# Column tiles of 320, 384 and 352 in place of three times 352, in a four-layer streaming encoder step

## The reference

```
layer 0 mixer: z = h @ w_in (1024 -> 2048); half of it a gated spatial mix,
               half a causal convolution of width 4 and a gated recurrence; @ w_out
layer 0 MLP:   square(relu(h @ up)) @ down        (1024 -> 4096 -> 1024)
layer 1 mixer: bg, cg, xv = split(h @ w_in, 3);   (bg * conv3(cg * xv)) @ w_out
layer 1 MLP:   as in layer 0
```

## Time and profile before

| | |
|---|---|
| median of 3 executions | 2187.01 us (2185.21 to 2187.84) |
| the profiled execution, its own time | 2186.56 us |
| its span | 2184.6 us |
| TensorE (PE) busy | 2168.7 us, 99% |
| VectorE (DVE) busy | 907.4 us, 42% |
| ScalarE (ACT) busy | 666.8 us, 31% |
| GpSimd (POOL) busy | 96.3 us, 4% |
| DMA | 142.99 MB, mean 65 GB/s |
| granted TensorE clock, mean | 0.998 of 2.4 GHz |

### The profile page before, as it was taken

One profiled execution on the slowest core, in us unless ns is written; L12 is line 12 of the kernel. 1 busy time (PEld: TensorE's weight loads), 2 busy tenths in 40 slices (PEclk: granted clock), 3 DMA queues, 4 the chain that ended last, 5 costly groups with the idle time before them and its releaser, 6 DMA issues.

```text
span 2184.6 us, 31823 instructions
## 1 busy us (share of the span) xinstructions
PE 2168.7 (99%) x13629; PEld 2154.2 (99%) x13629; DVE 907.4 (42%) x1431; ACT 666.8 (31%) x1137; POOL 96.3 (4%) x115
## 2 busy tenths in 40 slices
PE   9999999999999999999999999999999999999998
PEld 8999999999999999999999999999999999999997
DVE  5766358323322322334953333493223223322336
ACT  6664345202311320333511112453013103202333
POOL 1000000000000000000033231000000000000000
PEclk9999999999999999999999999999999999999999
DMA  6111422111111111132311114221111111111132
GB/s 218 49 41 39 138 75 83 49 47 41 49 49 49 41 48 49 49 110 67 119 49 41 47 49 138 69 81 56 49 42 47 49 49 47 41 49 49 55 122 80
DMA packets 228891, 142.99 MB, mean 65 GB/s; under 512 B 5248, under 2 KB 227408, under 8 KB 228752
## 3 DMA queue, kind: packets, MB, share of 16 engines
q1 hardware_dynamic: 228304, 140.89, 21.3%
q0 software_dynamic: 416, 0.07, 0.0%
q10 hardware_dynamic: 32, 0.01, 0.0%
HBM read 119.22 MB, written 21.73 MB: 65 GB/s over the span
## 4 chain that ended last, share of the span: by engine, by line
PE 88%; DVE 2%; issue 0%; ACT 0%; DVEq 0%; ACTq 0%
PE ps L679 29%; PE ps L680 29%; PE ps L682 29%; DVE x_lo L1383 1%; DVE x_old L1372 0%; DVE f L1355 0%; PE ps L781 0%; DVE f L1339 0%; DVE f L1347 0%; DVE f L1365 0%; DVE w_all L1306 0%; PE ps L719 0%; DVE f L1434 0%; ACT tmp L945 0%; PE ps L804 0%
## 5 line engine op out<-in xcount | busy, mean ns | idle before, releaser
L679 PE MATMUL ps<-x_hi,w_all 128*128 128x352 f32 x2328 | 757.6, 325 | 1.5 <-DVE x_lo L1383 1.5
L680 PE MATMUL ps<-x_lo,w_all 128*128 128x352 f32 x2328 | 748.5, 322 | 0.0
L682 PE MATMUL ps<-x_hi,w_all 128*128 128x352 f32 x2304 | 740.3, 321 | 0.0
L679 PE MATMUL ps<-h_hi,w_all 128*128 128x352 f32 x1728 | 556.5, 322 | 0.0
L682 PE MATMUL ps<-h_hi,w_all 128*128 128x352 f32 x1728 | 555.2, 321 | 0.0
L680 PE MATMUL ps<-h_lo,w_all 128*128 128x352 f32 x1728 | 555.2, 321 | 0.0
L679 PEld LDWEIGHTS ps<-x_hi,w_all 128*128 128x128 f32 x2328 | 437.5, 188 | 5.4 <-issue 2.0
L680 PEld LDWEIGHTS ps<-x_lo,w_all 128*128 128x128 f32 x2328 | 437.6, 188 | 2.2
L682 PEld LDWEIGHTS ps<-x_hi,w_all 128*128 128x128 f32 x2304 | 432.6, 188 | 0.0
L909 ACT CAST w_all<-w_all_raw 128x1024 fp32r<-128x1024 f32 x168 | 175.5, 1045 | 522.1 <-DMA w_all_raw<-in_mlp_down_dram 317.8
L679 PEld LDWEIGHTS ps<-h_hi,w_all 128*128 128x128 f32 x1728 | 324.4, 188 | 0.4 <-DVE h_lo L1595 0.3
(11 more groups left out here) (218 smaller groups left out, 1458.0 us busy)
## 6 DMA issues: line engine op xcount, KB each, us to landing
w_all_raw<-in_mlp_up_dram SPq DMA_DIRECT2D x60, 512.0 KB, 3.9
w_all_raw<-in_mlp_down_dram SPq DMA_DIRECT2D x60, 512.0 KB, 3.9
x_save<-f SPq DMA_DIRECT2D x12, 1408.0 KB, 6.4
x_old<-x_save SPq DMA_DIRECT2D x12, 1408.0 KB, 11.5
w_all_raw<-in_c_w_in_dram SPq DMA_DIRECT2D x22, 512.0 KB, 3.8
w_all_raw<-in_w_in_even_dram SPq DMA_DIRECT2D x15, 512.0 KB, 3.8
x_rows<-in_x_prompt_dram SPq DMA_DIRECT2D x8, 512.0 KB, 7.5
w_all_raw<-in_w_out_even_dram SPq DMA_DIRECT2D x6, 512.0 KB, 3.9
```

Of the source, the lines that this page charges most:

```text
L679: nc.tensor.matmul(dst, wh, hi, start=(i == 0), stop=False)
L680: nc.tensor.matmul(dst, wh, lo, start=False, stop=False)
L682: last = nc.tensor.matmul(dst, wl, hi, start=False, stop=(i == KC - 1))
```

## The change

The three tiles become 320, 384 and 352 columns wide and begin at 0, 320 and 704. All column ranges are taken from two tables. The tiles `tmp` grow to 384 columns; `caches` and the three `row_` buffers move to the spare columns of `x_old` (which lies where `x_lo` does), and the 32 bytes of padding behind `tmp` go. The views of the spare columns of `x_hi` become 32 wide. The weights of slot "hb" lie at the same columns as before (320 + 32 = 352 + 0). The core of the diff:

```diff
+TILE0, WIDTH = (0, 320, 704), (320, 384, 352)
+COLS = [slice(c, c + w) for c, w in zip(TILE0, WIDTH)]
...
-        tmp = [place(f"tmp{t}", [P, TT], F32) for t in range(3)]
-        at_byte[0] += 32
+        tmp = [place(f"tmp{t}", [P, max(WIDTH)], F32) for t in range(3)]
...
-        caches = place("caches", [P, CACHE_ROWS], F32)
...
-        row_sq = place("row_sq", [P, 9], F32)
-        row_root = place("row_root", [P, 9], F32)
-        row_rstd = place("row_rstd", [P, 9], F32)
...
-        spare = [x_hi_raw[:, k * TS + TOK:k * TS + TOK + NJ] for k in range(KC)]
+        spare = [x_hi_raw[:, k * TS + TOK:k * TS + TS] for k in range(KC)]
...
+        spare = [x_old[:, k * TS + TOK:k * TS + TS] for k in range(4)]
+        caches = spare[0][:, 0:CACHE_ROWS]
...
+        row_sq, row_root, row_rstd = [b[:, 0:9] for b in spare[1:4]]
...
         def pt(buf, c, t):
-            c0 = c * (buf.shape[1] // KC) + t * TT
-            return buf[:, c0:c0 + TT]
+            c0 = c * (buf.shape[1] // KC) + TILE0[t]
+            return buf[:, c0:c0 + WIDTH[t]]
...
-                c = (32, 0)[t]
+                c = 32
...
         def bank(n):
-            return ps[:, n % NB, 0:TT]
+            return ps[:, n % NB, 0:WIDTH[UNITS[n].t]]
...
-            n = P if s < 2 else TT - 2 * P
+            n = P if s < 2 else WIDTH[t] - 2 * P
```

More of the change, by code:

```diff
@@ L154, in tile_pieces @@
 def tile_pieces(t):
-    lo, hi = t * TT, (t + 1) * TT
+    lo, hi = COLS[t].start, COLS[t].stop
     if hi <= SEQ:
-        return [(0, TT, lo, False)]
+        return [(0, WIDTH[t], lo, False)]
     return [(0, SEQ - lo, lo, False), (SEQ - lo, hi - SEQ, SEQ, True)]
@@ L293, in pt, with part, rstd_wide @@
         def pt(buf, c, t):
-            c0 = c * (buf.shape[1] // KC) + t * TT
-            return buf[:, c0:c0 + TT]
[L297 to L301, removed]
+            c0 = c * (buf.shape[1] // KC) + TILE0[t]
+            return buf[:, c0:c0 + WIDTH[t]]
+        def part(buf, k0, k1, t, c0=0, c1=None):
+            return tiles3(buf)[:, k0:k1, TILE0[t] + c0:TILE0[t] + (c1 or WIDTH[t])]
+        def rstd_wide(t, n, c0=0, c1=None):
+            c1 = c1 or WIDTH[t]
+            return rstd[:, TILE0[t] + c0:TILE0[t] + c1].unsqueeze(1).to_broadcast([P, n, c1 - c0])
         def vec(i, rows=P):
@@ L345, in bank, with held @@
         def bank(n):
-            return ps[:, n % NB, 0:TT]
+            return ps[:, n % NB, 0:WIDTH[UNITS[n].t]]
+        def held(n):
+            return tmp[n % 3][:, 0:WIDTH[UNITS[n].t]]
         w_in = {s: sem(f"w_in_{s}") for s in SLOTS}
@@ L567, in _ @@
                 t, c0, n, rows = out_piece(i)
[L568 removed]
+                tok = TILE0[t] + c0
                 sp.wait_ge(o_a, i + 1)
@@ L718, in col_sums @@
                 wait(pe, rooted, n)
-                nc.tensor.matmul(ps[:, M0, 0:NJ], quads[:, :], fold[n % 6], start=True, stop=True
+                nc.tensor.matmul(ps[:, M0, 0:WIDTH[t] // QUAD], quads[:, :], fold[n % 6][:, 0:WIDTH[t] // QUAD], start=True, stop=True
                                  ).then_inc(col, 1)
@@ L789, in warm_up @@
             def warm_up(a):
-                nc.tensor.matmul(ps[:, a, 0:TT], tmp[0][:, 0:P], tmp[0][:, :], start=True, stop=True)
+                nc.tensor.matmul(ps[:, a, 0:TT], tmp[0][:, 0:P], tmp[0][:, 0:TT], start=True, stop=True)
             def keep_warm(a):
@@ L953, in out_unit @@
                     act.wait_ge(pe_unit, n + 1)
-                    nc.scalar.activation(tmp[n % 3][:, :], bank(n), ACT.Square).then_inc(f_sq, 1)
+                    nc.scalar.activation(held(n), bank(n), ACT.Square).then_inc(f_sq, 1)
                     nc.scalar.activation(pt(f, u.m, u.t), bank(n), ACT.Identity,
@@ L1396, in out_sum @@
                         dve.wait_ge(t_out, 16 * 6)
-                    nc.vector.tensor_copy(dst, tmp[n % 3][:, :]).then_inc(f_acc, 1)
+                    nc.vector.tensor_copy(dst, held(n)).then_inc(f_acc, 1)
                 else:
                     wait(dve, f_acc, i)
-                    nc.vector.tensor_tensor(dst, dst, tmp[n % 3][:, :], ALU.add).then_inc(f_acc, 1)
+                    nc.vector.tensor_tensor(dst, dst, held(n), ALU.add).then_inc(f_acc, 1)
             def h_low(n):
@@ L1427, in evacuate @@
                         dve.wait_ge(h_ready, i - 2)
-                    ins = nc.vector.scalar_tensor_tensor(tmp[n % 3][:, :], bank(n), 0.0, scale, ALU.max, ALU.mult)
+                    ins = nc.vector.scalar_tensor_tensor(held(n), bank(n), 0.0, scale, ALU.max, ALU.mult)
                 if u.kind == "dn0":
@@ L1463, in evacuate @@
                         dve.wait_ge(f_acc, 48)
-                    ins = nc.vector.tensor_tensor(tmp[n % 3][:, :], bank(n), factors(n), ALU.mult)
+                    ins = nc.vector.tensor_tensor(held(n), bank(n), factors(n), ALU.mult)
                 ins.then_inc(evac_d, 1)
```

53 lines of the change are left out of this document (27 added, 26 removed).

## The result

The kernel after takes 2216.48 us (median of 4; 2215.79 to 2217.02), the kernel before 2186.63 in the same comparison (2185.21 to 2187.84): ratio 1.0137, 95% interval 1.0125 to 1.015. It is 30 us slower, and the forecast was 2181.2 with a range up to 2197. Nothing in the busy times of the other engines explains it.

What follows compares the result with a forecast made beforehand. TensorE's matmul stream, busy 99%, was taken as the bound. Start -7.4 and turns +1.6 gave -5.8 us on the profiled 2186.56, so 2180.8; with the median 0.45 us above, 2181.2 us, range 2104 to 2197.

Steps and rivals of the forecast that it cites:

- Part 1, Width: TensorE's matmuls: the sum of widths stays 1056, so moving 32 columns from tile 0 to tile 1 costs nothing.
- 7.4 us more: Upper bound for width and start edits together, if the good tiles owed their saving to their half block.
- Part 2, Start: Tile 1 would begin at a multiple of 64 columns, saving 1.67 ns in each of 4416 triples: 7.4 us.
- B: Rival: in TensorE's stream a half block of 64 columns costs a whole one; 84 us saved, 2108.9 us; chance 0.20.
- C: Rival: matmuls of whole 64-column widths pay 13.3 ns surplus on tiles 0 and 1; slower, 2195.9 us; chance 0.13.
- Part 3, the turns: Where VectorE makes the next input, TensorE would wait for x_low, mainly tile 1 at 1076 us: 1.6 us lost.
- Parts 4, 6 and 7: Evacuations and low parts shift by some 0.05 us, covered; DMA nothing; start and end counted as nothing, within 0.4 us.
- Part 5: Small buffers moved with the same readers, and wider tmp: nothing, within 0.2 us.
- 3 ns over two passes: Plain float32 matmuls of 352 columns: a step of 0.297 us against 293.3 ns for two passes, so almost no surplus.
- D: Rival: no change; start doesn't matter or only the width sum counts (2188.6 us), or the turns eat the gain; chance 0.20.

Runs made afterwards that it cites:

- experiment 4: The kernel before, three tiles of 352 unchanged, with its activation buffers moved by 128 bytes (32 columns): 2193.78 us against 2185.95, ratio 1.0034.
- Experiment 2: The kernel after, its moved small buffers and wider tmp kept, with three tiles of 352 as before: 2189.63 us against 2185.79 for the kernel before, ratio 1.0015.
- experiment 5: TensorE's stream alone with shorter weights, bf16, other neighbours, three aligned tiles: 384 columns took 175.0 and 173.2 ns with weights of 64 and 32 columns, bf16 162.5.
- experiment 1: TensorE's stream alone, without the kernel's other work, at several widths and starts: the 320, 384, 352 panel averaged 11.61 us against 11.44 before.
- experiment 6: The kernel after with one more matmul of 128 columns ahead of each tile-2 unit, 184 in all: 2231.1 us, 14.6 above the kernel after.

## Why the prediction was wrong

**Part 1, Width, is the step that failed.** "If the surplus is one amount for each matmul, or one for each column, moving 32 columns from tile 0 to tile 1 costs nothing." It is neither. At 320 columns it is 13.3 ns where the forecast took 11.7, and on tile 1 at 384 it is 16.0. Against the forecast this is +6.7 us on tile 0 and +19.5 on tile 1, of the 37.3 between -7.4 and +29.9. The two distances alone, 1.67 and 4.3 ns by 4416, give 7.4 and 19.1. The unknown had been named and had one width to rest on; the bound of "7.4 us more" was no bound, since no row limited what 384 columns may cost.

**Part 2, Start.** Right for 352 columns (experiment 4: 6.9 us for 7.4), wrong as a rule for tiles: at 384 the sign turns (173.5 to 174.6 off a multiple, 176.0 at one). The change gave up the tile that the saving had been measured on.

**The third term wasn't in the sum: tile 2.** Its columns didn't change and its forecast was 158.3 ns. The last 11.1 us are its 61 units in the dearer of two states. The earlier trace rows with the earlier trace rows had shown that state, 167.0 ns on an aligned 352 tile, and the prediction used it as an argument within B and C and set it aside, since tiles 0 and 2 otherwise held 158.3. They held it in rows where every third tile was an unaligned one of 352 columns; the change took that tile away. Experiment 2 shows such a tile ending the dearer state three times; that it is what had kept it out is argued from that.

**Part 3, the turns.** The place and the mechanism were right (0.88 us at tile 1 of the second turn), the size was too large. Over the four tile-0 units TensorE came 1.12 us early, not 1.28, as 320 columns cost 146.7 ns; and VectorE's first `x_low` of tile 1 began 14.62 us behind the turn's first matmul where it had been 14.42, 0.2 us later and not 0.5. **Parts 4, 6 and 7** hold as far as the sums show: DVE's grew by 0.6%, and outside the stream 0.4 us changed. **Part 5** ("Nothing, within 0.2 us") doesn't: with the widths of before the moved buffers cost 3.8 us (experiment 2), by the state of 352 columns and not by their readers.

One reading was loose. The four plain float32 records of the earlier trace rows are two matmuls: `warm_up` issues two there, and the trace has two records for each. So 0.297 us is half of such a matmul. The sum that follows, 3 ns over two passes, holds for a record.

**The rivals.** C had the direction and the place, and for 320 the size: 146.7 ns. It put 384 at 173.3 and left tile 2 out, so 2195.9 instead of 2216. Its reason, a lock with the weight loads, isn't borne out by experiment 5 as far as their length goes. B falls with experiment 1, D with the result. The Trainium skill's rule ("TensorE: Matmul & The Clock Gate", section "Wait — 56ns, not 53.3ns?"), columns over 2.4 GHz and about 2.5 ns, agrees with bf16 here to 0.1 ns (149.2 at 352 columns) and doesn't hold for fp32r at full clock (146.7 to 176.0 ns against 135.8 to 162.5).

## What to carry to other kernels

Where TensorE's stream of fp32r matmuls is the bound, the distance of two starts is a property of width, start and neighbours, and must be measured for each of them: a stream of some dozens of matmuls in the kernel's own order gave the panel to 0.1 us in 11.6, where one width's surplus carried over to others missed by 26 us, and the state by 11 more. Such a short stream did not tell which state a long program falls in (experiment 6). A difference between two otherwise equal tiles is a fact about those tiles, and the change should be asked whether it keeps them. An odd value in one unit of a trace (167.0 where all others show 158.3) is a state that the next change may enter many times (here 61).

## What the runs showed that I had not expected

- 352 fp32r columns at a multiple of 64 have two states at full clock, 158.3 and 166.7 ns (380 and 400 cycles), each of which held for all the aligned matmuls that followed in one stream (576 and 360). From idle 2 of 6 pairs and 2 of 4 single units began in the dearer one. What in the engine holds the state stays open, and so does what the weights' place has to do with it.
- From 240 columns up the surplus of fp32r over the width ran from 24.6 to 48 cycles, that of bf16 was 6.0 at three widths. 128, 192 and 240 fp32r columns all take 111.7 ns, and there the weights' load is the nearest cause, which I only argue.
- Moving the activation buffers by 128 bytes, with every instruction the same, changed the time by 7.8 us, 0.34%.
